# 32 extra tokens in place of 16 in a mixture-of-rows layer: V rows gathered early and summed by TensorE in four column groups

## The reference

```python
def peer_ffn(h, wq, keys, u_tab, v_tab):          # h: 512 tokens x 1024
    ...                                           # blocks of 128 tokens
        q = (hc @ wq).reshape(PEER_BLOCK, PEER_HEADS, 2, PEER_DHALF)
        sc = jnp.einsum('thcd,hckd->thck', q, keys).astype(jnp.float32)
        s1, i1 = lax.top_k(sc[:, :, 0], PEER_TOPK)       # 16 of 128
        s2, i2 = lax.top_k(sc[:, :, 1], PEER_TOPK)
        ...                                              # 256 sums of pairs
        top, pos = lax.top_k(cand, PEER_TOPK)            # 16 of those
        eidx = jnp.take_along_axis(cidx, pos, axis=-1)
        gate = jax.nn.softmax(top, axis=-1)
        ue = jnp.take(u_tab, eidx, axis=0)               # 8 heads x 16 rows of 1024
        act = jax.nn.gelu(jnp.einsum('thkd,td->thk', ue, hc).astype(jnp.float32))
        ve = jnp.take(v_tab, eidx, axis=0)
        return jnp.einsum('thk,thkd->td', (gate * act).astype(ve.dtype), ve)
```

## Time and profile before

| | us |
|---|---|
| median of three runs | 3603.51 |
| lowest and highest | 3599.83, 3608.82 |
| profiled execution, its own time | 3608.11 |
| span of its instructions | 3606.4 |
| of it, PE busy | 3461.8 |
| DVE busy | 2999.9 |
| ACT busy | 1365.5 |
| POOL busy | 922.4 |

### The profile page before, as it was taken

How to read it: one execution, slowest core, us unless ns; L and a number is a source line. 1 busy time by engine, 2 the same in 40 slices (tenths; PEclk the granted TensorE clock), 3 DMA queues, 4 the chain that set the end, 5 groups by cost and what they waited for, 6 DMA issues and landing times. The chain is left out here.

```text
span 3606.4 us, 67692 instructions
## 1 busy us (share of the span) xinstructions
PE 3461.8 (96%) x27390; PEld 3190.9 (88%) x27390; DVE 2999.9 (83%) x5623; ACT 1365.5 (38%) x2110; POOL 922.4 (26%) x692
## 2 busy tenths in 40 slices
PE   8899899999999999999999989999999999999997
PEld 5679677999999998999987867799999999999997
DVE  8687575899989978888978757589998997888887
ACT  3541343433344433333344135343334443333333
POOL 2000000122221144656520000012222114465552
PEclk9999999999999999999999999999999999999999
DMA  7821431688888999999952043168888899999995
GB/s 234 300 92 27 125 117 55 204 281 269 277 284 271 291 347 370 369 369 382 378 211 82 20 132 112 59 197 282 268 279 283 275 293 340 372 373 371 381 361 209
DMA packets 387080, 896.38 MB, mean 249 GB/s; under 512 B 32976, under 2 KB 214352, under 8 KB 379984
## 3 DMA queue, kind: packets, MB, share of 16 engines
q1 hardware_dynamic: 302800, 590.00, 49.9%
q0 software_dynamic: 83968, 302.06, 22.5%
HBM read 772.85 MB, written 116.95 MB: 247 GB/s over the span
## 5 line engine op out<-in xcount | busy, mean ns | idle before, releaser
L2520 POOL DMA_INDIRECT row<-in_peer_u_rows,row_at x288 | 349.8, 1215 | 987.1 <-DVE row L2804 956.7
L228 PE MATMUL peer_ps<-peer_h_high,tile_high 128*128 128x368 f32 (+1 forms) x1504 | 502.7, 334 | 0.0
L230 PE MATMUL peer_ps<-peer_h_high,tile_low 128*128 128x368 f32 (+1 forms) x1504 | 500.2, 333 | 0.0
L229 PE MATMUL peer_ps<-peer_h_low,tile_high 128*128 128x368 f32 (+1 forms) x1504 | 500.2, 333 | 0.0
L228 PE MATMUL peer_ps<-gate_high,tile_high 128*128 128x368 f32 x1360 | 457.1, 336 | 36.3 <-DVE tile_low L221 35.7
L221 DVE TENSOR_TENSOR tile_low<-peer_tile,tile_high 128x1024 fp32r<-128x1024 f32 x362 | 441.1, 1220 | 58.7 <-ACT tile_high L216 55.8
L229 PE MATMUL peer_ps<-gate_low,tile_high 128*128 128x368 f32 x1360 | 453.0, 333 | 0.0
L230 PE MATMUL peer_ps<-gate_high,tile_low 128*128 128x368 f32 x1360 | 451.7, 332 | 0.0
L216 ACT ACTIVATE gate_high<-weighed 128x368 fp32r<-128x368 f32 x256 | 131.1, 512 | 711.4 <-DMA peer_tile<-in_peer_v 461.2
L216 ACT ACTIVATE tile_high<-peer_tile 128x1024 fp32r<-128x1024 f32 x362 | 379.5, 1049 | 0.0
L2520 POOL DMA_INDIRECT row<-in_peer_v,row_at x144 | 273.6, 1900 | 208.2 <-DVE h_own L2811 179.5
(11 more groups left out here) (565 smaller groups left out, 8060.6 us busy)
## 6 DMA issues: line engine op xcount, KB each, us to landing
peer_tile<-in_peer_u SPq DMA_DIRECT2D x256, 512.0 KB, 4.9
peer_tile<-in_peer_v SPq DMA_DIRECT2D x256, 512.0 KB, 6.8
gates<-gates_out SPq DMA_DIRECT2D x46, 1024.0 KB, 8.5
gates_in<-gates SPq DMA_DIRECT2D x32, 1472.0 KB, 10.8
acts<-up_act SPq DMA_DIRECT2D x220, 184.0 KB, 5.1
act_in<-acts SPq DMA_DIRECT2D x220, 184.0 KB, 7.7
in_w<-in_w_in SPq DMA_DIRECT2D x32, 512.0 KB, 3.6
peer_tile<-in_peer_wq SPq DMA_DIRECT2D x32, 512.0 KB, 5.0
```

Of the source, the lines that this page charges most:

```text
L228: pe.matmul(out, wh, mh, start=first, stop=False)
L229: pe.matmul(out, wh, ml, start=False, stop=False)
L230: return pe.matmul(out, wl, mh, start=False, stop=last)
L2520: pool.indirect_dma_start(row_of(n)[:, :], None, table, bass.IndirectOffsetOnAxis(ap=row_at[:, row_col(n):row_col(n) + 1], axis=0)) \
```

## The change

EXTRA becomes 32 with 4 partitions for each, so TD becomes 352, and GROUPS 22. An extra token now has 4 rows of each head to a partition: ROWS = 160 gathers of U, and 32 gathers of V beside the 128 for the own tokens. The 32 V rows of the extra tokens are taken from DVE: POOL gathers them in 8 rounds of 4 (`gather_parts`) into four buffers of their own, DVE makes four small stationary matrices of 32 columns a round (`make_stations`, the weights times a fold), and PE multiplies them with the four rows, each into its own 32 partitions of the banks 6 and 7 (`sum_parts`, 8 products a round), over all rounds without taking the sum out. ACT copies it to `extra_sum` at the last group. Three of the rounds are summed in the search, five in the spread, at places given in tables. For this the softmax of the gates is made for four heads at a time; the spread keeps four banks in place of six; U rows are taken at 14 a head, at 2 a tile in the tail, and in the first 8 tiles of down; V begins at tile 10.

```diff
-EXTRA, EX_PARTS = 16, 8
+EXTRA, EX_PARTS = 32, 4
...
-ROWS_BY_HEAD, ROWS_BY_GROUP, ROWS_BY_TILE = 13, 0.75, 0.8
-DOTS_UNTIL = 16
+PARTS = 4
+EX_ROUNDS = PH * EX_COLS // PARTS
+BATCH = PH // 2
+ROWS_BY_HEAD, ROWS_BY_GROUP, ROWS_BY_TILE = 14, 0.75, 2.0
+DOTS_UNTIL = 8
...
-GBANKS = 6
+GBANKS = 4
...
+PART_GATHER_AT = {42: 0, 79: 1, 88: 2, 96: 3, 108: 4, 111: 5, 114: 6, 117: 7}
+PART_STATIONS_AT = ({5: (0, 1), 6: (2,), 7: (3,)}, (3, 6, 9, 13), ((4,), (5,), (6,), (7,)))
+PART_SUMS_AT = {(6, 2): 0, (6, 9): 1, (7, 4): 2}
+PART_SUMS_IN_SPREAD = {0: 3, 4: 4, 8: 5, 11: 6, 15: 7}
...
+            def gather_parts(r):
+                if r:
+                    pool.wait_ge(part_summed.sem, part_summed.at(r))
+                for g in range(PARTS):
+                    j = OWN + PARTS * r + g
+                    pool.indirect_dma_start(part_row[g][:, :], None, dram_rows[1], bass.IndirectOffsetOnAxis(ap=row_at[:, j:j + 1], axis=0)) \
+                        .then_inc(part_loaded.sem, 16)
...
+                if n in PART_GATHER_AT:
+                    gather_parts(PART_GATHER_AT[n])
                 if n >= NROW:
                     pool.wait_ge(row_used.sem, row_used.at(n - NROW + 1))
...
+            def sum_parts(r):
+                pe.wait_ge(part_loaded.sem, part_loaded.at(16 * PARTS * (r + 1)))
+                pe.wait_ge(part_made.sem, part_made.at(r + 1))
+                for half in range(2):
+                    for g in range(PARTS):
+                        w = P // PARTS
+                        last = pe.matmul(ps[6 + half][w * g:w * g + w, :], stations[:, r % 2, g, :], part_row[g][:, half * T:(half + 1) * T],
+                                         start=(r == 0), stop=(r == EX_ROUNDS - 1))
+                last.then_inc(part_summed.sem, 1)
...
                 if hd:
-                    rows(min(rows_done[0] + 1, hd * ROWS_BY_HEAD))
+                    rows((hd - 1) * ROWS_BY_HEAD + ROWS_BY_HEAD * (done[0] - slot_start[0]) // (UPS_HEAD + 2))
...
+            def make_stations(r):
+                b = 2 * r // EX_ROUNDS
+                j = slice(OWN + PARTS * r, OWN + PARTS * (r + 1))
+                if r >= 2:
+                    dve.wait_ge(part_summed.sem, part_summed.at(r - 1))
+                dve.wait_ge(dots_gelued.sem, dots_gelued.at(b + 1))
+                dve.wait_ge(part_placed.sem, part_placed.at(16 * BATCH * (b + 1)))
+                link(dve.tensor_tensor(part_weights[:, r % 2, :], dots[:, j], own_gates[:, j], ALU.mult))
+                dve.tensor_tensor(stations[:, r % 2, :, :], fold[:, :].rearrange("p (g t) -> p g t", g=1).to_broadcast([P, PARTS, P // PARTS]),
+                                  part_weights[:, r % 2, :].rearrange("p (g t) -> p g t", t=1).to_broadcast([P, PARTS, P // PARTS]), ALU.mult) \
+                    .then_inc(part_made.sem, 1)
...
-                    rows(min(2 * ROWS, ROWS + ROWS * (e + 1 - adds) // (ROWS_END - adds)))
+                    rows(min(ROWS + OWN, ROWS + OWN * (e + 1 - adds) // (ROWS_END - adds)))
```

More of the change, by code:

```diff
@@ L2303, with row_order, head_of @@
 UPS_GROUP = lambda g: 1 + (g % 3 == 0)
+def row_order():
+    order, own = [], 0
+    for hd in range(PH):
+        first = min(hd * TOPK, own + ROWS_BY_HEAD // 2) if hd + 1 < PH else own
+        until = min((hd + 1) * TOPK, own + ROWS_BY_HEAD - EX_COLS) if hd + 1 < PH else OWN
+        order += [*range(own, first), *(OWN + hd * EX_COLS + j for j in range(EX_COLS)), *range(first, until)]
+        own = until
+    return order
+ROW_ORDER = row_order()
+DOTTED_EXTRA = [ROW_ORDER.index(OWN + BATCH * (b + 1) * EX_COLS - 1) + 1 for b in range(2)]
+PART_GATES_AT = (63, 105)
+PART_GATHER_AT = {42: 0, 79: 1, 88: 2, 96: 3, 108: 4, 111: 5, 114: 6, 117: 7}
+PART_STATIONS_AT = ({5: (0, 1), 6: (2,), 7: (3,)}, (3, 6, 9, 13), ((4,), (5,), (6,), (7,)))
+PART_SUMS_AT = {(6, 2): 0, (6, 9): 1, (7, 4): 2}
+PART_SUMS_IN_SPREAD = {0: 3, 4: 4, 8: 5, 11: 6, 15: 7}
 def row_col(n):
-    hd, i = divmod(n % ROWS, HEAD_ROWS)
-    return hd * TOPK + i if i < TOPK else OWN + hd * EX_COLS + i - TOPK
+    return ROW_ORDER[n] if n < ROWS else n - ROWS
+def head_of(n):
+    j = ROW_ORDER[n]
+    return j // TOPK if j < OWN else (j - OWN) // EX_COLS
 def stream_order():
@@ L2351, in peer @@
     extra_placed = pg.counts("extra_placed")
+    part_loaded, part_made, part_summed, part_placed = (pg.counts(f"part_{n}") for n in ("loaded", "made", "summed", "placed"))
     own_turned, h_flipped = pg.counts("turned"), pg.counts("h_flipped")
@@ L2383, in peer @@
         row_atf = buf("row_atf", [P, 2, TOPK])
-        extra_at, extra_gates, fold = buf("extra_at", [P, OWN], U32), buf("extra_gates", [P, OWN]), buf("extra_fold", [P, EXTRA])
+        extra_at, extra_gates, fold = buf("extra_at", [P, OWN], U32), buf("extra_gates", [P, OWN]), buf("extra_fold", [P, P // PARTS])
+        fold_back, part_weights = buf("extra_fold_back", [P, EXTRA]), buf("part_weights", [P, 2, PARTS])
+        stations = buf("part_stations", [P, 2, PARTS, P // PARTS])
+        part_row = [pg.placed(f"part_row{b}", [P, D], F32, 212960 + 4096 * b) for b in range(PARTS)]
         row = [buf(f"row{b}", [P, D]) for b in range(NROW)]
@@ L2497, in _, with place @@
         def _(pool):
-            for n in range(2 * ROWS):
+            heads_known = [0]
+            def place(into, source, k):
+                return pool.dma_start(into[:, OWN + k * EX_COLS:OWN + (k + 1) * EX_COLS],
+                                      source[EX_AT:P, k * TOPK:(k + 1) * TOPK].rearrange("t (q k) -> t q k", q=EX_PARTS))
+            def gather_parts(r):
[5 more added lines that the diff above has]
+                        .then_inc(part_loaded.sem, 16)
@@ L2507, in _ @@
-                if n < ROWS and i == TOPK:
+                    place(row_at, extra_at, hd).then_inc(extra_placed.sem, 16)
                     pool.wait_ge(extra_placed.sem, extra_placed.at(16 * (hd + 1)))
-                if n == ROWS - 2:
-                    pool.wait_ge(found.sem, found.at(1))
-                    for k in range(PH):
-                        pool.dma_start(own_gates[:, OWN + k * EX_COLS:OWN + (k + 1) * EX_COLS],
-                                       extra_gates[EX_AT:P, k * TOPK:(k + 1) * TOPK].rearrange("t (q k) -> t q k", q=EX_PARTS)) \
-                            .then_inc(extra_placed.sem, 16)
+                    heads_known[0] = hd + 1
@@ L2515, in _ @@
+                if n in PART_GATES_AT:
+                    b = PART_GATES_AT.index(n)
+                    pool.wait_ge(found.sem, found.at(b + 1))
+                    for k in range(BATCH * b, BATCH * (b + 1)):
+                        place(own_gates, extra_gates, k).then_inc(part_placed.sem, 16)
+                if n in PART_GATHER_AT:
+                    gather_parts(PART_GATHER_AT[n])
                 if n >= NROW:
@@ L2731, in _ @@
                     step(m)
+                if g == PART_STATIONS_AT[1][0] - 1:
+                    extra_gelu(1)
+                if g == GROUPS - 1:
+                    act.wait_ge(part_summed.sem, part_summed.at(EX_ROUNDS))
+                    for j in range(2):
+                        act.activation(extra_sum[:, j * T:(j + 1) * T], ps[6 + j][:, :], ACT.Copy)
                 take_gates(g)
@@ L3052, in peer @@
         slab_loaded[s % NSLAB].passed(16)
-    for n in range(2 * ROWS):
+    for n in range(ROWS + OWN):
         row_loaded[n % NROW].passed(16)
```

113 lines of the change are left out of this document (72 added, 41 removed).

## The result

The changed kernel takes 3567.2 us in the median (3562.08 to 3568.91), beside 3606.16 us for the kernel before (the three runs listed further up and one more, of 3617.43); the ratio is 0.9894, with a 95% interval of 0.9872 to 0.9915. That is 39 us less, where 59 were forecast: the direction and the range held, and the size was two thirds of the forecast.

The account below looks back on a forecast made before the run. PE was taken to pace the search, PE and DVE the spread, PE and DMA tail and down. Terms -2.6 + 0 - 1 - 26 = -29.6 us a layer, -59 for two, gave 3545 us; range 3485 to 3605.

Parts of the forecast that it names:

- PE's pace: PE's time for one tile: 4.00 us at 368 columns, 3.84 us at 352, so 0.16 us less a tile.
- First head and bridge, -2.6: 10 tiles of U and 6 of the bridge, paced by PE, each 0.16 us shorter: -2.6 us a layer.
- Seven heads, 0: Search: DVE takes the pace from PE and the PE gain is spent: 0 us a layer, bounds -6 and +6.
- A round at 0.87 us: PE's price for one round of eight sums in column groups, 0.43 us for each four; 2.6 us for three.
- Spread, -1: 22 groups at DVE's 8.25 us save 5.5 us, less 4.5 for DMA: -1 us a layer, bounds -6 and +8.
- The 4.5 us added for the DMA engines: Spread: DMA needs 9.2 us a group in groups 1 to 12, above DVE's 8.25; half the excess, some hidden.
- Tail and down, -26: 596 us become 570, 205.6 MB in place of 215 at 361 GB/s: -26 us a layer, bounds -10 and -38.
- the latency rival: Down stays at 4.27 us a tile whatever it moves; tail 68 us, first eight tiles 37; 3638 us, chance 0.07.
- Full pace: Rival: everything keeps pace with PE, search gains 9 us, tail and down 38; 3489 us, chance 0.15.
- take turns: Rival: column groups run one after another, a round costs 3.4 us, +41 us in all; 3586 us, chance 0.05.
- The rule of the Trainium skill that was weighed above: A weight load overlaps running matmuls only when the row group differs, so a round would expose its loads; forecast followed the trace.
- at their limit at 280 and 290 GB/s: Rival: DMA already limits search and spread, adding 54 and 21 us there, +46 a layer; 3696 us, chance 0.05.

## Why the prediction was right in its direction, and where it failed

*PE's pace.* 4.00 to 3.84 us a tile was right: starts of products of 352 columns are 160 ns apart in the search and in down, where those of 368 were 167.

*First head and bridge, -2.6.* Measured: -1.3 and -1.3 us to the 14th low part, -0.6 and +0.7 in the bridge; -1.2 a layer. The first head gave most of its 1.6 us, the bridge nothing.

*Seven heads, 0.* Measured +10.2 and +9.7, outside its bounds of -6 to +6. This is the step that failed most. DVE's work was worked out as 361.6 us and is 361.3; I had written that 7.7 us of small gaps stay, which makes 369, and yet took 366, the time of before, on the thought that DVE's lead would hide the rest. There is no lead to be had for an engine that is the slowest through 84 tiles. The other 7 us over 369 are mostly waits that I had let shrink to nothing or not grow: 3.7 us for rows at the start, where it was 1.7, and 4.1 us for ACT's high parts, of the 16.0 of before. The longest of these stands here:

```profile
849.02 0.47 ACT L2716 ACTIVATE up_act<-peer_ps 128x352 f32<-128x352 f32 x1 [4.14 <-DMA acts<-up_act]
849.38 1.05 ACT L216 ACTIVATE tile_high<-peer_tile 128x1024 fp32r<-128x1024 f32 x1
850.47 1.23 DVE L221 TENSOR_TENSOR tile_low<-peer_tile,tile_high 128x1024 fp32r<-128x1024 f32 x1 [2.89 <-ACT tile_high L216]
```

ACT waits for its stores to land, just behind the first round's gathers (POOL issues the last at 835.7 us) and 125 us ahead of the first sum (975.6), so the gathers and not the products hold this one up. The kernel that keeps only the first round's gathers has a wait of 1.8 us at the same, 50th, low part (847.8 us), the one without rounds has 0.3 us in the whole window. Of the 10 us, the experiment without rounds takes away 6; the one with 12 rows a head takes 13.

*A round at 0.87 us.* It is 1.9 us. I read sixteen instructions in the earlier trace rows as sixteen products; the loop at that line writes eight, as `sum_parts` does, and each appears twice in the trace. The whole row, 1.92 us, was the price of a round. It did little harm, since the search had PE time to spare and in the spread it only brought PE level with DVE: 27 tiles, 20 times 2.73 us of one-hots and 4 rounds at 1.86 are 165.7 us for PE, and the window is 165.4.

*Spread, -1.* Measured from the 105th to the 132nd low part, 163.8 to 165.4: +1.6 for the same 27 tiles, and -6.9 for the group that is gone, -5.3 in all. DVE's 8.25 us a group was the right figure (165.4 us for the 27 tiles' 20 groups, 8.27). The 4.5 us added for the DMA engines were not paid. They now move 338 GB/s there where they moved 290, with no wait of DVE for a tile or a row; so not all of the busy time that I had counted for each byte was needed.

*Tail and down, -26.* From the tail's start 594.1 and 593.1 before, 572.7 and 564.8 after, 566.9 and 578.8 in the repetition: -23 in the mean, within the bounds. The bytes came out: 205.0 MB by the three windows of the result, where 205.6 were counted, at 358 GB/s. But that the DMA engines at 361 GB/s set the time is the part that the runs don't bear out, and the close figure is in part luck. 14 rows less to move gave nothing back, the same bytes in the old places took 9 us more, and 32 tokens alone moved 370 GB/s for 481 us. By stretches, DVE is full in the first eight tiles (37.2 us), and PE is busy 461.6 of 468.3 us in the other 120, 3.90 us each. The forecast took the DMA figure over PE's 538 us; what the whole exceeds it by lies mostly in the tail, 67 us for 12 tiles, and in the first eight, both as the latency rival had them (68 and 37).

*The rivals.* Full pace fell with DVE in the search; in the last 120 tiles of down it came near. The column groups do not take turns: 16 instructions in 1.9 us are 0.12 each, four at a time. The rule of the Trainium skill that was weighed above (TensorE: Matmul & The Clock Gate, "Part 3: Packing small matmuls — row/col tiling") again does not describe this form: the loads of the round shown above run beside its products with all rows in use. The pace of down is not pure latency, since fewer rows a tile shortened it (4.30 us at 1.36, 4.1 at 1.21, 3.95 at 1.12; at 1.08, with 16 rows a head, it stays at 3.95 to 4.02), and ACT's wait for tiles of V stayed long (next row, 1370 to 1838 us) with PE busy 98.6%. The DMA engines are not at their limit at 280 and 290 GB/s: they moved 311 and 338.

```profile
ACT gate_high L216 <- DMA peer_tile<-in_peer_v: 213.7, 73, 7.9
```

Sum: -1.2 + 9.9 - 5.3 - 23 = -19.6 us a layer, -39 for two, which is what the medians show. Against the forecast's -29.6 the first head and the bridge are 1 short, the search is 10 short, the spread 4 better, tail and down 3 short.

## What to carry to other kernels

When an added piece of work makes another engine the slowest of a stage, the stage takes that engine's work plus its unavoidable gaps; the old time of the stage is no floor and no estimate. Work that can be taken in several stages should be priced in each of them, and only the first part of it is cheap there: 14 rows a head was worth it and 16 was not. Before a wait is moved forward in a queue, count what stands behind it.
